# Expert weights in eight areas of half a unit, and the second block's first columns taken into the last down unit

## The reference

```
u2 = modulate(rmsnorm(h, norm_ffn_g), sh2, sc2)
h = h + g2 * hier_moe(u2, ...)      # silu(x @ w_gate) * (x @ w_up) * gate, then @ w_down, 16 experts, FF 256
x = rmsnorm(h, norm_final_g)        # end of the first block
proj = rmsnorm_2(x, norm_gain) @ w_in_2   # second block: bq, bf, bi, aq, ak, ...
```

## Time and profile before

| what | value |
|---|---|
| median of 3 runs | 698.34 us (696.48 to 699.16) |
| profiled execution | 698.22 us, its span 696.9 us |
| TensorE, DVE, ACT busy | 664.0, 464.2, 354.1 us |
| read from memory | 162.37 MB, 235 GB/s over the span |

### The profile page before, as it was taken

One profiled execution on the slowest core, in us unless ns is written; L12 is line 12 of the kernel. 1 busy time (PEld: TensorE's weight loads), 2 busy tenths in 40 slices (PEclk: granted clock), 3 DMA queues, 4 the chain that ended last, 5 costly groups with the idle time before them and its releaser, 6 DMA issues.

```text
span 696.9 us, 10461 instructions
## 1 busy us (share of the span) xinstructions
PE 664.0 (95%) x4082; PEld 467.4 (67%) x4082; DVE 464.2 (67%) x830; ACT 354.1 (51%) x568; POOL 65.4 (9%) x74
## 2 busy tenths in 40 slices
PE   3999999999999999998979799989999999999997
PEld 1877666676888878743323222479888897888886
DVE  1546898654678867584655455797988666756754
ACT  2344523674634445476556556558244467753442
POOL 0002120305001000000000001001005301300000
PEclk9999999999999999999999999999999999999999
DMA  9999688849525955679999999835444665545541
GB/s 285 351 269 393 231 295 322 318 174 381 200 93 180 327 216 177 221 241 361 298 366 317 348 308 374 286 91 180 122 139 134 183 211 152 180 151 183 179 121 60
DMA packets 108991, 164.14 MB, mean 236 GB/s; under 512 B 10896, under 2 KB 53613, under 8 KB 108814
## 3 DMA queue, kind: packets, MB, share of 16 engines
q1 hardware_dynamic: 107038, 155.58, 67.2%
q0 software_dynamic: 1904, 7.90, 3.3%
HBM read 162.37 MB, written 1.08 MB: 235 GB/s over the span
## 4 chain that ended last, share of the span: by engine, by line
PE 77%; DMA 8%; DVE 7%; ACT 3%; SPq 3%; issue 1%; POOL 1%; ACTq 0%; DVEq 0%; POOLq 0%
PE p L634 18%; PE p L636 17%; PE p L635 17%; PE p L1157 10%; DMA s_WX<-in_w_exp_up_dram 3%; DMA s_WX<-in_w_exp_down_dram 3%; PE p L703 2%; PE p L692 2%; PE p L1312 2%; SPq L502 2%; DVE s_rawr L1929 1%; DMA s_GS<-in_w_ada_dram 1%; DMA s_raw<-in_w_in_dram 1%; PE p L749 1%; POOL s_L L575 1%
## 5 line engine op out<-in xcount | busy, mean ns | idle before, releaser
L1482 ACT ACTIVATE s_hi<-s_raw 128x1024 fp32r<-128x1024 f32 x144 | 149.0, 1055 | 119.5 <-PE p L636 56.5
L1929 DVE TENSOR_TENSOR s_rawr<-s_raw,s_hi 128x1024 fp32r<-128x1024 f32 x144 | 177.4, 1246 | 39.1 <-ACT s_hi L1482 38.7
L634 PE MATMUL p<-s_hi,s_Ah 128*128 128x512 f32 (+1 forms) x384 | 154.2, 402 | 0.5 <-DVE s_Al L1948 0.3
L636 PE MATMUL p<-s_hi,s_Al 128*128 128x512 f32 (+1 forms) x384 | 148.4, 387 | 0.0
L635 PE MATMUL p<-s_rawr,s_Ah 128*128 128x512 f32 (+1 forms) x384 | 148.3, 386 | 0.0
L634 PEld LDWEIGHTS p<-s_hi,s_Ah 128*128 128x128 f32 x384 | 72.2, 188 | 26.2 <-issue 7.2
L636 PEld LDWEIGHTS p<-s_hi,s_Al 128*128 128x128 f32 x384 | 72.2, 188 | 15.1
L635 PEld LDWEIGHTS p<-s_rawr,s_Ah 128*128 128x128 f32 x384 | 72.4, 188 | 12.7
L2435 DVE COPY s_put<-s_WX 128x512 f32 x120 | 44.1, 421 | 40.7 <-DMA s_WX<-in_w_exp_up_dram 19.0
L1743 ACT ACTIVATE s_put<-s_WX 128x512 f32 x72 | 40.0, 619 | 43.2 <-DMA s_WX<-in_w_exp_up_dram 20.7
L1157 PE MATMUL p<-s_WX,s_XG 128*32 128x512 f32 x256 | 50.9, 613 | 10.5 <-DVE s_hid L2485 8.0
(11 more groups left out here) (401 smaller groups left out, 1047.1 us busy)
## 6 DMA issues: line engine op xcount, KB each, us to landing
...
```

Of the source, the lines that this page charges most:

```text
L634: pe.matmul(o, xh, wh, start=start, stop=False)
L636: return pe.matmul(o, xl, wh, start=False, stop=stop)
L1482: act.activation(T.hi[:, i % NHL, :], T.raw[:, i % NRAW, :], ACT.Copy).then_inc(*S.hi(i))
L1929: dve.tensor_tensor(T.lo[:, i % NRAW, :], T.raw[:, i % NRAW, :], T.hi[:, i % NHL, :].bitcast(F32), ALU.subtract).then_inc(*S.lo_dve(i))
```

## The change

The expert stage's weights get eight areas of 1 MB: six in `WX` and one each in `L` and `T12`, which are free in that stage. The areas rotate by halves (`AREAS`), with the last half in area 3 once more. A half holds one k of all four groups and is fetched by two transfers of 512 KB (up) or one of 1 MB (down); it waits for the half that used the area before (`area_free`). Rounds and copies wait for their half alone. The `pl` pieces go into the memory of B. The masks come as bytes straight into their place, issued earlier. In ACT and DVE silu and `hidden` stand ahead of `put(v, 0)`. The last down units are ordered down 2 c0, down 3 c0, down 2 c1, down 3 c1; `rows_out(., 0)` moves to unit 22, `rows_back(., 0)` ahead of unit 23, the turns for the first 512 columns into unit 23 and bq 0 ahead of `rows_back(., 1)`. All 1024 columns of X3 come by `rows_in`. bq uses banks PZ[0] and PM[0]. The diff, cut:

```diff
-UNITS += [("up", 3, h) for h in range(4)] + [("down", e, c) for e in (2, 3) for c in range(2)]
+UNITS += [("up", 3, h) for h in range(4)] + [("down", e, c) for c in range(2) for e in (2, 3)]
+DOWNS = [u[1:] for u in UNITS if u[0] == "down"]
...
+AREAS = (3, 0, "L", 5, 1, 4, 2, "T12")
+AREA = [AREAS[m % 8] for m in range(2 * LAST + 2)]
+AREA[-1] = 3
+AREA_BEFORE = [max((n for n in range(m) if AREA[n] == a), default=None) for m, a in enumerate(AREA)]
...
-    T.WX = over("WX", [128, 12, HC])
+    T.WX = over("WX", [128, 24, 512])
...
-    T.Bh, T.Bl = sb("Bh", [128, 8, 256], F32R), sb("Bl", [128, 8, 256], F32R)
+    T.PLH = nc.alloc_sbuf_tensor_at("s_PLH", [128, 2, HC], F32R, offset=-(-nc.sbuf_base // 32) * 32)
+    T.Bh = sb("Bh", [128, 8, 256], F32R)
+    T.PLR = over("PLR", [128, 2, HC])
+    T.PLL = nc.alloc_sbuf_tensor_at("s_PLL", [128, 2, HC], F32R, offset=-(-nc.sbuf_base // 32) * 32)
+    T.Bl = sb("Bl", [128, 8, 256], F32R)
     T.HT = over("HT", [128, 2, 2, 352])
...
-    T.gain, T.gated = T.BI[:, 1024:2048], T.YR[:, 0:512]
+    T.gain, T.gated = T.BI[:, 1024:2048], T.YR[:, 0:1024]
...
+def raw_place(T, i):
+
+    return T.PLR[:, PIECES[i][1], :] if PIECES[i][0] == "pl" else T.raw[:, i % NRAW, :]
...
-    return (T.PM if half else T.PZ[2:4])[tt]
+    return ((T.PZ[1], T.PM[1]) if half else T.PZ[2:4])[tt]
...
+def bq_banks(T):
+
+    return [T.PZ[0], T.PM[0]]
...
+def half_done(S, m):
+
+    return S.round.at(m // 2, m % 2, 2)
...
 def raw_free(S, i):
 
     first = AT["bq", 0]
+    if PIECES[i][0] == "pl":
+        return S.piece.at("ro1", 3, 1)
     if first <= i < first + NRAW:
-        return unit_done(S, LAST - 2 + i % NRAW // 4)
+        return half_done(S, AREA_LAST[i % NRAW // 2])
     return piece_done(S, i - NRAW)
...
+def area_free(S, v, j):
+
+    m = 2 * v + j
+    if AREA_BEFORE[m] is not None:
+        return half_done(S, AREA_BEFORE[m])
+    a, end = AREA[m], AT["pl", 0]
+    if a == "L":
+        return ada_used(S, 21)
+    if a == "T12":
+        return ada_used(S, 22)
+    if a < 4:
+        return piece_done(S, max(i for i in range(end) if i % NRAW in (2 * a, 2 * a + 1)))
+    return piece_done(S, max(i for i in range(end) if i % NHL in (2 * a - 8, 2 * a - 7)))
+
...
+def half_parts(I, v, j, w):
 
     kind, e, h = UNITS[v]
-    w = r.rearrange("p (k n) -> p k n", k=2)
     if kind == "up":
-        a, b = (I[name][4 * g + e].rearrange("(k p) n -> p k n", p=128)[:, 2 * h:2 * h + 2] for name in ("w_exp_gate", "w_exp_up"))
+        a, b = (I[name].rearrange("(g e) (k p) n -> p e k g n", g=4, p=128)[:, e, 2 * h + j] for name in ("w_exp_gate", "w_exp_up"))
         return [(w[:, :, 0:256], a), (w[:, :, 256:512], b)]
-    return [(w, I["w_exp_down"][4 * g + e].rearrange("(k p) n -> p k n", p=128)[:, :, 512 * h:512 * h + 512])]
+    return [(w, I["w_exp_down"].rearrange("(g e) (k p) n -> p e k g n", g=4, p=128)[:, e, j, :, 512 * h:512 * h + 512])]
 
 
...
+    sp.dma_start(T.masks[:, :, :], I["masks"].rearrange("p (l t) -> p l t", l=8)).then_inc(*S.masks_in(0))
     pieces(AT["pl", 0] - done[0])
...
-    unit(0, range(4))
-    unit(1, (0, 1))
-    unit(2, (2, 3))
-    q.wait_ge(*S.dve_res.at("x", 1, 1))
-    sp.dma_start(T.G1[:, :], I["masks"]).then_inc(*S.masks_in(0))
+    def half(v, j):
+        q.wait_ge(*area_free(S, v, j))
+        for dst, src in half_parts(I, v, j, area(T, v, j)):
+            sp.dma_start(dst, src).then_inc(*S.half_in[AREA[2 * v + j]](v, j))
+
+    for v in range(4):
+        half(v, 0)
+        half(v, 1)
     q.wait_ge(*ada_used(S, 23))
     sp.dma_start(T.BI[:, 1024:2048], I["norm_final_g"].rearrange("(a n) -> a n", a=1).broadcast_to([128, 1024])).then_inc(*S.final_gain_in(0))
-    unit(1, (2, 3))
-    unit(2, (0, 1))
-    for v in range(3, LAST + 1):
-        unit(v, range(4))
+    for v in range(4, LAST + 1):
+        half(v, 0)
+        half(v, 1)
     pieces(len(PIECES) - done[0])
...
                 q.wait_ge(*S.dve_moe.at("ht", e))
-                if j == 0 and (e or c):
-                    q.wait_ge(*S.dve_moe.at("y2", e - 1 + c, 1 - c))
+                n = DOWNS.index((e, c))
+                if j == 0 and n:
+                    q.wait_ge(*S.dve_moe.at("y2", *DOWNS[n - 1]))
...
+    down(3, 0)
     down(2, 1)
-    down(3, 0)
-    down(3, 1)
     q.wait_ge(*S.act_moe.at("ht", 3))
     q.wait_ge(*S.dve_moe.at("ht", 3))
     for s in range(3):
         rows_back(s, 0)
+
+    def u3_into(b, k0):
+        T.turn_bank["u3", k0] = b
+        q.wait_ge(*S.dve_moe.at("x3", k0 // 2, 1))
+        for k in range(2):
+            for tt in range(2):
+                r = pe.transpose(PT[b][:, 256 * k + 128 * tt:256 * k + 128 * tt + 128], T.X3[:, tt, 128 * (k0 + k):128 * (k0 + k) + 128], ident)
+        r.then_inc(*S.turned("u3", k0))
+
+    def u3_cols(k0):
+        q.wait_ge(*S.dve_moe.at("x3", k0 // 2, 1))
+        turn(lambda tt, k: T.X3[:, tt, 128 * k:128 * k + 128], ("u3", k0), S.dve_cols.at("u3", k0))
+
+    def u3(h):
+        return "u3", 2 * h
+
+    down_half(3, 1, 0)
+    q.wait_ge(*S.dve_rows.at("lo", 0, 0))
+    u3_into(0, 0)
+    q.wait_ge(*S.dve_moe.at("hid", 3, 2))
+    u3_into(2, 2)
+    down_half(3, 1, 1)
+    m_free[0] = S.dve_cols.at("u3", 2)
+    z_free[0] = [S.dve_rows.at("lo", 1, 0)]
+    t_free[0], t_free[1] = S.dve_cols.at("u3", 0), S.dve_rows.at("lo", 0, 1)
+    uses("bq", 0, 1, A, u3, turned=True, banks=bq_banks(T))
+    q.wait_ge(*S.dve_rows.at("lo", 1, 1))
     q.wait_ge(*S.dve_moe.at("y2", 3, 1))
     for s in range(3):
         rows_back(s, 1)
-    m_free[0] = m_free[1] = S.dve_moe.at("gy", 1, 1)
-    z_free[0] = z_free[1] = [S.dve_rows.at("lo", 1, 1)]
+    z_free[1] = [S.dve_moe.at("gy", 1, 0)]
+    m_free[1] = S.dve_moe.at("gy", 1, 1)
     z_free[2] = z_free[3] = [S.dve_moe.at("gy", 0, 1)]
-    t_free[0] = t_free[1] = S.dve_rows.at("lo", 0, 1)
-
-
-    def u3_cols(k0):
-        q.wait_ge(*S.dve_moe.at("x3", min(k0 // 2, 2), 1))
-        turn(lambda tt, k: T.X3[:, tt, 128 * k:128 * k + 128], ("u3", k0), S.dve_cols.at("u3", k0))
-
-    def u3(h):
-        return "u3", 2 * h
-
-    u3_cols(0), u3_cols(2)
-    uses("bq", 0, 1, A, u3, turned=True)
-    u3_cols(4)
-    uses("bq", 1, 2, A, u3, turned=True)
-    u3_cols(6)
-    uses("bq", 2, 4, A, u3, turned=True)
-    chunk_freed("bq", S.dve_hgrn.at("bq", 0), S.dve_hgrn.at("bq", 1))
+    uses("bq", 1, 2, A, u3, turned=True, banks=bq_banks(T))
+    u3_cols(4), u3_cols(6)
+    uses("bq", 2, 4, A, u3, turned=True, banks=bq_banks(T))
+    z_free[0], m_free[0] = [S.dve_hgrn.at("bq", 0)], S.dve_hgrn.at("bq", 1)
     uses("bf", 0, 2, A, u3, turned=True)
...
     for v in range(1, LAST + 1):
-        put(v, 0)
         kind, e, h = UNITS[v - 1]
         if (kind, h) == ("up", 3):
             silu(e)
+        put(v, 0)
         if v == 1:
             q.wait_ge(*S.dve_route.at("ev"))
             act.activation(ev, ev, ACT.Exp).then_inc(*S.act_route("ev"))
-        if v == LAST:
+        if v == LAST - 1:
             rows_out(0, 0), rows_out(1, 0)
         put(v, 1)
         if (kind, h) == ("up", 3):
             hid_cols(e)
-        if v == LAST:
+        if v == LAST - 1:
             rows_out(2, 0)
-    rows_out(0, 1), rows_out(1, 1), rows_out(2, 1)
+    cols_scaled("u3", 0, T.Ah, T.g_in2)
+    his_to(AT["bq", 1])
+    cols_scaled("u3", 2, T.Ah, T.g_in2)
+    rows_out(0, 1), rows_out(1, 1)
     his_to(AT["bq", 2])
+    rows_out(2, 1)
 
 
     def sums(key, src, junk, c, n, tt):
-        q.wait_ge(*S.dve_moe.at(*((key, n + 1, tt) if key == "x3" else (key, n, tt))))
+        q.wait_ge(*S.dve_moe.at(*((key, 2 * n + 1, tt) if key == "x3" else (key, n, tt))))
         squares(S.act_moe, ("sq " + key,), src, junk, c, n, tt)
 
...
     for v in range(4, LAST + 1):
-        put(v, 0)
         if UNITS[v - 1][0::2] == ("up", 3):
             hidden(UNITS[v - 1][1])
+        put(v, 0)
         if UNITS[v - 1][0] == "down":
             last_rows(*UNITS[v - 1][1:])
         if UNITS[v - 2][0::2] == ("up", 3):
             hid_cols(UNITS[v - 2][1])
-        if v == LAST:
-            rows_out(0, 0)
+        if v == LAST - 1:
+            rows_out(0, 0), rows_out(1, 0)
         put(v, 1)
-        if v == LAST:
-            rows_out(1, 0), rows_out(2, 0)
+        if v == LAST - 1:
+            rows_out(2, 0)
         if v == 7:
             q.wait_ge(*S.masks_in.at(0))
-            dve.tensor_copy(T.masks[:, :, :], T.G1[:, :].rearrange("p (l t) -> p l t", l=8)).then_inc(*S.dve_moe("masks"))
...
-            dve.tensor_tensor(T.gated, T.G2[:, 0:512], T.gain[:, 0:512], ALU.mult).then_inc(*S.dve_moe("gated gain"))
+            dve.tensor_tensor(T.gated, T.G2[:, :], T.gain, ALU.mult).then_inc(*S.dve_moe("gated gain"))
             for tt in range(2):
-                dve.tensor_tensor(T.X3[:, tt, 0:512], T.X[:, tt, 0:512], T.gain[:, 0:512], ALU.mult).then_inc(*S.dve_moe("gained"))
+                dve.tensor_tensor(T.X3[:, tt, :], T.X[:, tt, :], T.gain, ALU.mult).then_inc(*S.dve_moe("gained"))
+
...
+    def rows_in(j, tt):
```

(83 more changed lines are left out.)

46 lines of the change are left out of this document (15 added, 31 removed).

## The result

The changed kernel takes 689.8 us (median of 4 runs, 689.68 to 690.18) against 698.75 us for the kernel before on the same chip (4 runs, 696.48 to 699.17): a ratio of 0.988, 95% interval 0.986 to 0.990, so 1.2% faster and clear of the noise. The forecast was 690.1. The profiled execution has a span of 688.5 us, forecast 688.7, at full clock throughout.

A forecast was written before the change was run, and what follows sets the result against it. TensorE, busy 95% of the span, was taken as the bound, stalled by late expert weights. Unit 22 ending 8.2 us earlier and 0.0 from the way out give span 688.7, plus 1.3: 690.1 us; range 685.5 to 695.

The forecast's parts named there:

- (1): Expert stage: eight half-unit areas, four units deep, remove all waits for data and the late copies behind them; slack never below 11 us.
- the one stretch of 1.5 us: Unit 16: granted clock at 0.65 cost 1.5 us; the sum removes it; rival that low clock stays: 691.6, chance 0.12.
- (2): Silu and hidden rows ahead of copies: new waits for DVE's copies, 2.0 at expert 0 and three of 1.6, together 6.8 us.
- 124.6: Expert stage: time in us of the 23 units before the last one without waits, at 5.12 each plus extras.
- (3): Unit 8: gain multiplied in for 1024 columns instead of 512, mask cast gone; costs nothing, bounds 0 and 2 us.
- (4): Last down units reordered: rows out in unit 22 delay DVE's copies 0.3 us; unit 22 ends at 431.9, 8.2 us earlier.
- (5): Way out, from unit 22's end to bf3: 38.6 us before and after, so 0.0 gained; bounds -4.5 and +4.
- the three waits foreseen: Way out: TensorE's idle saved before bq0 comes back in front of bq2, bq3 and bf0.
- The transfers' size: Expert weights: larger transfers would only add slack, leaving the sum unchanged.
- a slower rival: Expert transfers: gathering from four experts brings the rate under 300 GB/s, giving 702 us; chance 0.05.

The follow-up runs named there:

- e9: Changed kernel with silu and hidden rows behind the copies again, plus a one-element Silu on ACT ahead of unit 4's copies: 684.31 us.

## Why the prediction was right

**(1) The areas.** Forecast: all waits for transfers go. They did, with the late copies behind them and the low clock (1.00 at 398). The last half was asked for at 418.45, when its area came free, not when the queue had time, so it landed later than forecast (about 427, with the 8.6 us that a down half takes, for 421), and TensorE came to it only at 439.44. For unit 10 the slack was some 9 us and not 14: its first half was asked for at 338.96 and, with the median of 8.1 us to landing, there by about 347.5, where the forecast had 343 (an estimate). The rates taken, 350 and 380, are those of the trace: 348 to 350 GB/s in the windows from 364 to 400, 386 in those from 404 to 416. The depth of four units, from which the forecast drew its slack, was not needed: six areas do as well in this kernel, and cost 1.1 us in the one without the order's wait.

The clock was part of it beyond the one stretch of 1.5 us that the forecast took from a single trace. In the 42 executions of the kernel before that ran beside the experiments the mean granted clock was 0.990 to 0.998, in the change's four 0.999 to 1.0. No run separates what of the gain is clock.

**(2) The order.** Forecast 6.8 us in four waits. Measured 6.6: four units of 8.0 us for 6.35. (The view of waits, in which the ends of matmuls are modelled, gives 5.9 for them.) The 7.3 us that unit 22 is late over 124.6 are these 6.6, the 0.6 by which 20 units at 5.15 us are longer than at 5.12, a small error of the forecast's sum, and 0.1 at the last down units. The place and the mechanism were DVE's copies, as the run with ACT's silu first shows. One part was off: expert 0 costs 1.65 us, no more than the others and not 2.0, since its table load (318.46) runs while TensorE is still in unit 3; the other three, forecast at 1.6, also take 1.65. Against the old order the price is 4.1 us, as that keeps 2.5 of its own: 1.8 behind expert 0, of which e9 gives 1.4 to the table load, which there has no cover, 0.3 each in front of units 10 and 16, and 0.1 at the end.

**(3) Unit 8** cost nothing, as forecast. **(4)** Rows out ahead of unit 22's late copies: forecast 0.3, measured 0.1: the loads of the second half wait 0.5 us for DVE's copy at 430.63, but from 428.85 to the sums at 432.47 are 3.62 us, where the same stretch of unit 1 took 3.52.

**(5) The way out.** Forecast 0.0, with bf3 38.6 after unit 22. Measured 38.1 in the profile, and 0.1 us by the run with the old way out. Of the three waits foreseen, those in front of bq2 and bf0 are there with 1.36 and 1.61; that of bq3 is not. The reason given, that TensorE's saved idle comes back because DVE has as much to do, has this for it, that taking the wait in front of bf0 away by DVE's order brought another behind the norm.

**The transfers' size.** The forecast had the larger transfers cost nothing and win nothing, and priced a slower rival at 702 if the rate fell under 300 GB/s. Both are seen: nothing at 256 KB for 512, and 702.5 us where small transfers held the up windows at 240 to 278. That this came from SyncE's 0.475 us per issue and not from the gathering was no part of the rival. The Trainium skill, "DMA: Bandwidth & Descriptors", section "Measured (HBM→SBUF, 128 partitions, SWDGE, issued from GpSimd)", asks for 1 MiB or more a transfer; on this queue, issued from SyncE, 256 KB gave 348 to 358 GB/s and one of 128 KB was held by its issue.

The sum was right through parts that were each near, but that the span came within 0.2 us is luck: unit 22 ended 0.4 later than forecast (start 0.2, longer units 0.6, less 0.2 each behind the experts and at the end), and the way out was 0.5 shorter. What it could not say is that one part of the change, the order, works against it: the forecast added the new order's four waits to a sum without late data, and never priced the areas with the order left out. That kernel is 4.1 us faster.
